# A decoder's attention, one head at a time, rewritten for pairs of heads

## The reference

```
moba (6 heads): softmax(q k^T / 8, causal) v          # with 256 tokens every key lies in the own block
nsa  (4 heads): g0 * softmax(q kc^T / 8) vc           # 15 compressed keys
              + g1 * softmax(q ks^T / 8, causal) vs   # all heads share one ks, vs
              + g2 * softmax(q kw^T / 8, causal) vw   # and one kw, vw
fox  (6 heads): softmax(q k^T / 8 + c_t - c_s, causal) v,  c = cumsum(log_sigmoid(f))
y = g_moba * (o_moba * silu(z)) W_moba + ... ;  x = x + y W_out
```

## Time and profile before

| | |
|---|---|
| runs | 2040.57 us median of 3 (2038.38 to 2041.07) |
| profiled execution | 2038.23 us, of which 2036.4 us from first to last instruction |
| PE busy | 1941.9 us (95%) |
| PE weight loads | 1804.3 us (89%) |
| DVE busy | 1271.0 us (62%) |
| ACT busy | 968.9 us (48%) |
| granted TensorE clock | 0.991 in the mean |
| HBM read | 299.30 MB |

### The profile page before, as it was taken

How to read it: one execution, slowest core, us unless ns; L and a number is a source line. 1 busy time by engine, 2 the same in 40 slices (tenths; PEclk the granted TensorE clock), 3 DMA queues, 4 the chain that set the end, 5 groups by cost and what they waited for, 6 DMA issues and landing times.

```text
span 2036.4 us, 35117 instructions
## 1 busy us (share of the span) xinstructions
PE 1941.9 (95%) x14810; PEld 1804.3 (89%) x14810; DVE 1271.0 (62%) x2087; ACT 968.9 (48%) x1481; POOL 79.2 (4%) x68
## 2 busy tenths in 40 slices
PE   7999997988999999999979889999999999999999
PEld 7999995887999999999868879999988779988779
DVE  6766575454666567665843646665764778753776
ACT  5544555244544444455552445444553544643542
POOL 0000101300000000000013000000000000000000
PEclk9999998999999999999989999999999999999999
DMA  8555431222555655554312325555446325446222
GB/s 319 187 185 187 156 125 62 81 96 94 176 186 182 207 182 186 183 187 156 117 63 82 105 84 176 185 184 187 158 146 205 97 72 170 155 153 202 87 76 101
DMA packets 84461, 302.63 MB, mean 149 GB/s; under 512 B 9168, under 2 KB 11728, under 8 KB 84176
## 3 DMA queue, kind: packets, MB, share of 16 engines
q1 hardware_dynamic: 84304, 300.39, 44.4%
HBM read 299.30 MB, written 1.05 MB: 147 GB/s over the span
## 4 chain that ended last, share of the span: by engine, by line
PE 88%; DVE 7%; ACT 2%; issue 2%; DMA 0%; SPq 0%; DVEq 0%; ACTq 0%
PE bank L383 22%; PE bank L387 22%; PE bank L386 22%; PE bank L663 3%; PE bank L401 2%; PE bank L404 2%; PE bank L405 2%; DVE w_lo L1458 1%; PE bank L843 1%; PE bank L956 1%; PE bank L448 1%; PE bank L452 1%; PE bank L453 1%; PE bank L778 1%; PE bank L921 1%
## 5 line engine op out<-in xcount | busy, mean ns | idle before, releaser
L383 PE MATMUL bank<-xs,w_hi 128*128 128x256 f32 x2576 | 737.8, 286 | 4.1 <-issue 4.1
L387 PE MATMUL bank<-xs,w_lo 128*128 128x256 f32 x2576 | 724.6, 281 | 0.0
L386 PE MATMUL bank<-xs,w_hi 128*128 128x256 f32 x2576 | 724.5, 281 | 0.0
L1031 ACT ACTIVATE w_hi<-ring 128x1024 fp32r<-128x1024 f32 x544 | 565.4, 1052 | 330.8 <-PE bank L383 258.7
L1458 DVE TENSOR_TENSOR w_lo<-ring,w_hi 128x1024 fp32r<-128x1024 f32 x544 | 653.5, 1235 | 103.9 <-ACT w_hi L1031 103.0
L383 PEld LDWEIGHTS bank<-xs,w_hi 128*128 128x128 f32 x2576 | 487.9, 189 | 24.4 <-issue 20.5
L386 PEld LDWEIGHTS bank<-xs,w_hi 128*128 128x128 f32 x2576 | 487.9, 189 | 3.2 <-issue 2.9
L387 PEld LDWEIGHTS bank<-xs,w_lo 128*128 128x128 f32 x2576 | 487.7, 189 | 0.0
L383 PE MATMUL bank<-a,w_hi 128*128 128x256 f32 x704 | 196.9, 280 | 0.0
L387 PE MATMUL bank<-a,w_lo 128*128 128x256 f32 x704 | 196.6, 279 | 0.0
L386 PE MATMUL bank<-a,w_hi 128*128 128x256 f32 x704 | 196.4, 279 | 0.0
(11 more groups left out here) (398 smaller groups left out, 3138.6 us busy)
## 6 DMA issues: line engine op xcount, KB each, us to landing
ring<-in_w SPq DMA_DIRECT2D x560, 512.0 KB, 3.3
arena<-in_mem SPq DMA_DIRECT2D x2, 1024.0 KB, 12.9
const<-in_const SPq DMA_DIRECT2D x1, 1647.0 KB, 16.2
h<-in_x SPq DMA_DIRECT2D x1, 768.0 KB, 7.5
out<-h SPq DMA_DIRECT2D x3, 256.0 KB, 2.3
dec_par<-in_dec SPq DMA_DIRECT2D x1, 615.0 KB, 19.9
h<-in_x SPq DMA_DIRECT2D x1, 256.0 KB, 3.9
out<-h SPq DMA_DIRECT2D x2, 128.0 KB, 1.9
```

The source lines that it names most:

```text
L383: last = nc.tensor.matmul(o, wh, hi(x, k0 + k), start=k == 0, stop=False, skip_group_check=True)
L386: nc.tensor.matmul(o, wh, lo(x, k0 + k), start=False, stop=False, skip_group_check=True)
L387: last = nc.tensor.matmul(o, wl, hi(x, k0 + k), start=False, stop=k == nk - 1, skip_group_check=True)
L1031: nc.scalar.activation(w_hi[:, s * UNIT:(s + 1) * UNIT], ring[:, u % RU, :], AF.Copy).then_inc(sems("w_hi"), 1)
```

## The change

The 20 units become 10 `PAIRED`, two heads each; nsa pairs share their keys.

- PE: `scores(i)` writes two neighbouring banks, first both heads' 256-key part and then both heads' 128-key part. For fox, four passes of rounded float32 over 64 rows add the forget sums (`rows_r` picks one head's row of `forget_r`, its high part in one group of 32 partitions and its low part in the next). Then two passes with the identity as stationary add the causal mask in PSUM. `turn` writes the turned weights over the scores in the same banks, both heads. `values` writes both halves of one bank, the two heads alternating. Scores of pair i wait until the turned weights of pair i-2 are copied. One filler step comes before `turn`, the others after it, and `values(i-1)` follows in the same iteration (before, it came one later). The compressed weights are turned in two visits, i = 1 and 4, in bank 7. `forget_rows` goes.
- ACT: one copy of both heads' turned weights (768 columns) first, then four exponentials straight out of PSUM with the scale 0.125, then `ptc`, high parts, tanh. Three copies per layer make the rounded constants; the copy of the forget sums has 256 columns instead of 12.
- DVE: no pass from PSUM to `s2`; two maxima over both heads straight out of PSUM, one sign, one reciprocal, two multiplications over both heads with a broadcast factor. Ahead of the loop four small scalings of the log forgets per layer, one memset in the first, and two subtractions of 32 partitions by 256 columns between `gates(1)` and `kcn`.
- POOL: its 18 operations per layer go. No DMA is added or removed but for a constant table that is smaller by 120 columns.

The names of semaphores are dealt out anew (left out here), the mask's sign is turned round, and a table `two32` is added to the constants. Lines that only "..." stands for are those removed, which the listing above shows, and unchanged ones.

```diff
@@ -194,7 +195,8 @@
-        bank = [ctx.enter_context(nc.psum_tensor(f"bank{i}", [P, 512], F32)) for i in range(8)]
+        banks = ctx.enter_context(nc.psum_tensor("bank", [P, 8, 512], F32))
+        bank = [banks[:, i, :] for i in range(8)]
@@ -319,6 +321,7 @@
+        forget_r = rounded("forget", T, arena_at + 4 * at[0])
@@ -326,14 +329,17 @@
+        mx2, nm2, sm2, rc2 = take(2, 4), take(2, 4), take(2, 4), take(2, 4)
+        gf, gate, xg, lf, lf2 = take(2, 18), take(2, 12), take(2, 6), take(2, 6), take(2, P)
...
+        p2, pt2 = take(2, 2, TRI), take(2, 2, TRI)
+        ident_r, causal_r, rows_r = (rounded(f"attend{n}", n, arena_at + 4 * (at[0] + o))
+                                     for o, n in ((0, P), (P, T), (P + T, 6 * P)))
+        take(7 * P + T)
@@ -882,10 +888,11 @@
+                nc.tensor.matmul(bank[4][:, 0:P], lf2[:, 0, :], le, start=True, stop=True, skip_group_check=True)
+                nc.tensor.matmul(bank[4][:, P:T], lf2[:, 0, :], ones, start=True, stop=False, skip_group_check=True)
+                nc.tensor.matmul(bank[4][:, P:T], lf2[:, 1, :], le, start=False, stop=True,
@@ -908,85 +915,99 @@
                         if j >= NH - 2 and t == 1:
                             last.then_inc(*pe.tell('cs_full'))
                 filler()
...
+                pe.e.wait_ge(*pe.need('masks', 3))
                 def scores(i):
...
+                    kind, q, k, _, tile = PAIRED[i][:5]
+                    b = 2 + i % 2 * 2
                     if i >= 2:
...
+                        pe.e.wait_ge(*pe.need('pt', i - 1))
+                    if i == 1:
+                        pe.e.wait_ge(*pe.need('fcol', 2))
+                        pe.e.wait_ge(*pe.need('kcs_ln', 1))
+                    Q, K = qn[:, q, :], qn[:, k, :]
+                    for t in (1, 0):
+                        for u in range(2):
+                            o = u * 64
+                            nc.tensor.matmul(bank[b + u][:, (1 - t) * T:(1 - t) * T + P + t * P],
+                                Q[o:o + 64, t * P:(t + 1) * P], K[o:o + 64, 0:P + t * P], start=t == 1, stop=False,
+                                skip_group_check=True)
+                    if kind == "fox":
+                        for t in range(2):
+                            for u in range(2):
+                                o, head = u * 64, (2 * (tile - 5) + u) * P
+                                nc.tensor.matmul(bank[b + u][:, t * T:(t + 1) * T], rows_r[o:o + 64, head:head + P],
+                                    forget_r[o:o + 64, :], start=False, stop=False, skip_group_check=True)
+                    for u in range(2):
+                        last = nc.tensor.matmul(bank[b + u][:, P:TRI], ident_r[:, :], causal_r[:, :], start=False,
+                            stop=True, skip_group_check=True)
+                    last.then_inc(*pe.tell('s_full'))
+                def turn(i):
+                    b = 2 + i % 2 * 2
+                    pe.e.wait_ge(*pe.need('pn', 2 * i + 2))
+                    for u in range(2):
+                        p = p2[:, i % 2, u, :]
+                        for c, at_ in ((T, 0), (0, P), (P, T)):
+                            last = nc.tensor.transpose(bank[b + u][:, at_:at_ + P], p[:, c:c + P], ident)
+                    last.then_inc(*pe.tell('t_full'))
+                def turn_compressed(j):
+                    pe.e.wait_ge(*pe.need('pcn', 1))
                     if j:
...
+                        pe.e.wait_ge(*pe.need('ob', 2))
+                    for u in range(2):
+                        for t in range(2):
+                            last = nc.tensor.transpose(bank[7][0:NCMP, u * T + t * P:u * T + (t + 1) * P],
+                                pc[:, 4 * j + 2 * u + t, :], ident)
+                    last.then_inc(*pe.tell('ct_full'))
                 def values(i):
...
+                    kind, _, _, vcols, tile, first, last = PAIRED[i]
+                    if i == 1:
+                        pe.e.wait_ge(*pe.need('ptc', 1))
                     pe.e.wait_ge(*pe.need('pt', i + 1))
                     b = 6 + tile % 2
...
+                    if tile >= 2 and first:
                         pe.e.wait_ge(*pe.need('ob', tile - 1))
...
+                    v, half = fv if kind == "fox" else v2, [bank[b][u * 64:u * 64 + 64, :] for u in range(2)]
                     if first and kind == "nsa":
...
+                        pe.e.wait_ge(*pe.need('ptc', 2))
+                        for u in range(2):
+                            nc.tensor.matmul(half[u][:, 0:T], vc[0:NCMP, :], ptc[0:NCMP, 2 * (tile - 3) + u, :], start=True,
+                                stop=False, skip_group_check=True)
+                    for t in range(2):
+                        for u in range(2):
+                            end = nc.tensor.matmul(half[u][:, t * P:T], v[:, t, vcols[u]:vcols[u] + 64],
+                                pt2[:, i % 2, u, t * T:t * T + T - t * P], start=t == 0 and first and kind != "nsa",
+                                stop=t == 1 and last, skip_group_check=True)
+                    end.then_inc(*pe.tell('o_full' if last else 'o_part'))
+                n = len(PAIRED)
+                for i in range(n + 1):
                     if i < n:
                         scores(i)
...
+                    steps = gate_steps(i + 1) - gate_steps(i)
+                    filler(1)
+                    if i >= 1:
                         turn(i - 1)
...
+                    filler(steps - 1)
+                    if i in (1, 4):
+                        turn_compressed(i // 4)
+                    if i >= 1:
+                        values(i - 1)
+                up_banks = (2, 3, 4, 5)
                 for m, (j, br, _) in enumerate(UPS):
                     first, nk = UP_TILES[br]
                     pe.e.wait_ge(*pe.need('ob', first + nk))
                     if m >= 4:
                         pe.e.wait_ge(*pe.need('up_out', m - 3))
...
+                    project(pe, w, ob, nk, up_banks[m % 4], "up_full", k0=first)
                 for j, b in enumerate(OUT_BANKS):
                     if j < 2:
                         pe.e.wait_ge(*pe.need('gl_e', 11 + j))
@@ -1304,6 +1325,9 @@
+                for r, c in ((ident_r[:, :], ident), (causal_r[:, :], C("causal")),
+                             (tiles(rows_r[:, :], 6), spread(C("two32")[:, 0:6], P))):
+                    nc.scalar.activation(r, c, AF.Copy).then_inc(*a.tell('masks'))
@@ -1346,7 +1370,7 @@
+                nc.scalar.activation(forget_r[:, :], bank[4][:, 0:T], AF.Copy).then_inc(*a.tell('forget_hi'))
@@ -1364,29 +1388,28 @@
                 a.e.wait_ge(*a.need('pc_d', 1))
                 nc.scalar.activation(pc, pc, AF.Exp).then_inc(*a.tell('pc_e'))
                 s.ahead(u0 + U_GL + 8)
...
+                n = len(PAIRED)
                 for i in range(n + 1):
...
                     if i >= 1:
...
+                        j, b = i - 1, 2 + (i - 1) % 2 * 2
                         a.e.wait_ge(*a.need('t_full', j + 1))
                         if j >= 2:
                             a.e.wait_ge(*a.need(*used_pt(j - 2)))
...
+                        nc.scalar.activation(pt2[:, j % 2, :, :], banks[:, b:b + 2, 0:TRI], AF.Copy).then_inc(*a.tell('pt'))
+                    if i < n:
+                        s_, b = i % 2, 2 + i % 2 * 2
+                        a.e.wait_ge(*a.need('nm', i + 1))
+                        for u in range(2):
+                            for t in (1, 0):
+                                x, k = slice((1 - t) * T, (1 - t) * T + P + t * P), 2 * t + u
+                                nc.scalar.activation(p2[:, s_, u, x], bank[b + u][:, x], AF.Exp, bias=nm2[:, s_, k:k + 1],
+                                    scale=0.125, accum_out=sm2[:, s_, k:k + 1]).then_inc(*a.tell('p'))
+                    if i in (1, 4):
+                        j = i // 4
+                        a.e.wait_ge(*a.need('ct_full', j + 1))
+                        nc.scalar.activation(ptc[0:NCMP, 2 * j:2 * j + 2, :], tiles(bank[7][0:NCMP, :], 2),
+                            AF.Copy).then_inc(*a.tell('ptc'))
+                    s.ahead(u0 + U_GL + 8 + gate_steps(i + 1) // 2)
                     for j in range(gates_turned(i), gates_turned(i + 1)):
                         gate_tanh(j)
                 for j in range(gates_turned(n + 1), 12):
@@ -1841,7 +1862,13 @@
+                    op1=ALU.subtract).then_inc(*d.tell())
+                if l == 0:
+                    nc.vector.memset(lf2, 0.0).then_inc(*d.tell())
+                d.e.wait_ge(*d.own())
+                for c in range(4):
+                    nc.vector.tensor_scalar(lf2[:, :, 32 * c:32 * c + 6], lf, -8.0, None,
+                        ALU.mult).then_inc(*d.tell('lf' if c == 3 else None))
@@ -1860,6 +1887,10 @@
+                d.e.wait_ge(*d.need('forget_hi', 1))
+                for o in (32, 96):
```

(27 more changed lines are left out.)

171 lines of the change are left out of this document (17 added, 154 removed).

## The result

The changed kernel takes 1977.47 us (median of 4 runs, 1974.92 to 1980.21) where the kernel before takes 2040.13 in the same comparison: a ratio of 0.9694, 95% interval 0.9677 to 0.9711, 62.7 us less. The profiled execution spans 1976.6 us against 2036.4, 59.8 less where my sum had 45.6; so 14 of the 17 us are looked for in the two traces (the other 3 are the distance between those two executions and the medians).

The account below looks back on a forecast made before the run. PE was taken to bound the kernel, attention stages included. Terms -32.4 - 6.3 - 2.3 + 0.4 + 1.2 - 6.2 = -45.6 from 2038.2 gave 1992.6, a median of 1995 us, range 1982 to 2016.

Parts of the forecast that it names:

- PE's waits: Attention stages, PE waiting for `turn` and `ptc`: 3.2 us per layer in place of 6.3, -6.2 us; bounds -12.6 to 0.
- pairs, forget sums, compressed keys, small transposes: PE's attention work: pairs -32.4 us, forget sums -6.3, compressed keys -2.3, small transposes in two visits +0.4.
- `kcn`: Two DVE subtractions between `gates(1)` and L1864 keep PE waiting: 0 to 0.8 us per layer, 0.6 taken, +1.2.
- all else outside the stages: Constants' copies, memset, small scalings, POOL and DMA: taken as 0; copies and scalings without cover 2 us per layer.
- The PE terms: PE's attention work: 2.74 us per pair of heads against 4.36, 1.62 less, 20 pairs, -32.4; without overlap -6.8.
- L905: Trace place with neighbouring products in two 64-row halves, read as two streams at full pace: 16 passes end in 1.09 us.
- The 0.21 that I worked out from it: First rival, passes start in program order: 0.21 us more for each `scores` and `values`, +9.3, 2004 us; chance 0.10.
- forecast of 1.0: Iterations 2 and 6: DVE's `gates` awaits ACT's high part, multiplications end 10.55, `turn` due 9.56; 1.0 us each.
- "0" for the constant table: Constants' copies ahead of PE: covered by units made ahead, so 0; the smaller table's shift of later tensors got no term.
- Everything outside the two stages within 2 us: Sign to check in the trace: outside the two attention stages, times would stay within 2 us of before.
- Rival 5: Attention ring through ACT and DVE, exponentials and maxima 1.6 times dearer from PSUM: +64, 2059 us, slower than before; chance 0.03.
- 6 us of waits off and 7 on: The main case's own range around its 1995 us, from PE's waits, given as 1987 to 2002.

## Why the prediction was right, and where it failed

The result, 1977.47, lies below the range, which ended at 1982. Two terms put it there: "PE's waits", 7.0 us too small, and the place of the operands, which I gave no price and which is worth some 8. Without the part of either that I missed, the time would have lain inside the range.

| term, us for both layers | forecast | from the traces |
|---|---|---|
| pairs, forget sums, compressed keys, small transposes | -40.6 | -40.6, a remainder (55.8 of the stages less 13.2 and 2) |
| waits of `turn` and `ptc` | -6.2 | -13.2 |
| the stages by the place of operands | 0 | about -2 |
| `kcn` | +1.2 | +1.9 |
| all else outside the stages | 0 | -6.0 in the profiled execution |
| sum | -45.6 | -59.9 (spans: -59.8) |

**The PE terms held.** The two choices that decided the size, full overlap of row halves (from L905) and of column halves (for which no row spoke), were right: 0.86 and 0.80 per pair where one head costs 0.84 and 0.79. That -40.6 comes out to the tenth is partly luck: it is a remainder, and what is taken off it is known to about 1 us; what holds is the terms per pair above. For the columns the forecast was a guess from the rows, and it came out. The passes start in pairs less than 0.01 us apart. The rule of the Trainium skill that I set against L905 says that matmuls start and end in program order ("TensorE: Matmul & The Clock Gate", section "Part 3: Packing small matmuls"). The 0.21 that I worked out from it for each `scores` and `values` is in neither trace. The records don't name the half of a pass or its place in the program, so they show that my working from the rule was wrong, and leave open what is in order.

**Failed: "PE's waits", the term of -6.2.** It went wrong at both ends. The old waits I took from the idle row, 6.3 per layer; from start to start they were 7.75, and the run with only DVE's order changed gave back 7.8. Idle time ahead of a matmul is not what the wait costs when the end of the pass before is modelled 0.16 us behind the next pass's usual start (0.28 us long, the next 0.12 behind it). The new waits I forecast at 3.2 per layer (two of 1.0 for `turn`, 0.3 for the last `turn`, 0.9 for `ptc`); they were 1.1 (0.29 for one `turn`, 0.84 for `ptc`). The mechanism in iteration 2 is as I described it, a gate projection between the exponentials and the multiplications, but each step is shorter. ACT and DVE there:

```profile
1597.44 0.48 ACT L1405 ACTIVATE arena<-bank,arena 128x256 f32<-128x256 f32 x1
...
1597.89 0.38 ACT L1405 ACTIVATE arena<-bank,arena 128x128 f32<-128x128 f32 x1
...
1598.23 2.02 ACT L1052 ACTIVATE w_hi<-ring 128x1024 fp32r<-128x1024 f32 x2
1599.34 1.22 DVE L1479 TENSOR_TENSOR w_lo<-ring,w_hi 128x1024 fp32r<-128x1024 f32 x1 [1.93 <-ACT w_hi L1052]
...
1600.48 0.68 DVE L1885 TENSOR_TENSOR arena<-bank,rstd 128x512 f32<-128x512 f32 x1
...
1601.09 0.17 DVE L1936 RECIPROCAL arena<-arena 128x4 f32<-128x4 f32 x1
1601.29 1.03 DVE L1945 TENSOR_TENSOR arena<-arena 128x512 f32<-128x512 f32 x2
```

A part of 256 and one of 128 columns take 0.79 from start to start (1597.44 to 1598.23), so four take 1.58, where I took 1.8 to 2.0; the reciprocal and the multiplications 1.14 (1601.09 to 1602.23, where the maxima start) instead of 1.35 with the gate. Instructions on ACT and DVE start up to 0.1 us before the one ahead has ended by its row (the four exponentials add up to 1.70 and take 1.58, the reads of their row sums included), and I had added durations whole. Iteration 2 begins at 1592.53. Its exponentials end 5.7 behind that instead of 6.25 and the multiplications 9.8 instead of 10.55, while `turn` was due at 9.55, as I had said. So the forecast of 1.0 became 0.29 in iteration 2 and nothing in iteration 6. Together the waits are 7.0 of the 14.3 that my sum was short.

**Failed: "0" for the constant table.** I mentioned among the DMAs that it gets smaller, and gave it no price. That it moves every operand behind it was in the diff and nowhere in the sum. The sign that I had named, "Everything outside the two stages within 2 us", failed: it was 6.0 apart from `kcn`. The kernel before, moved by 32 bytes, is 9.0 us faster, and its stages 0.4 and 0.6 shorter with waits 0.4 and 0.6 longer, so 2 us by pace inside them. Measured from that kernel, at 512 bytes' distance, the rewrite itself gives 2029.24 - 1977.47 = 51.8 us, and my sum with the waits and `kcn` put right gives 45.6 + 7.0 - 0.7 = 51.9. By the ratios of the two comparisons the first figure is 53.6, so they agree within 2 us, and the 0.1 is luck. Outside the stages the profiled executions differ by 6.0 apart from `kcn`, where the moved kernel's trace has 8.5; the rest is within what one execution differs from the next (the changed kernel's encoder ends at 1432.0 in one and 1427.3 in the other). That a shift of 512 bytes changes nothing by itself was not tried, and since place isn't all that moves the decoder's pace, the 6.0 is the likely price of the place, not a shown one.

**`kcn`** I took at 0.6 per layer between 0 and 0.8; it is 0.9: the two subtractions (0.88 us together in the trace) start at 1567.13, when ACT's logarithm and exponential have ended (1567.05), so these cover none of them. **`ptc`** came out as said. Rival 5's assumption, dearer exponentials out of PSUM, had the wrong sign. One slip: my own range, "6 us of waits off and 7 on", is 1989 to 2002 around 1995, not 1987 to 2002.

## What to carry to other kernels

Two products that each use half of TensorE's rows or columns cost here as much as one (0.86 against 0.84 us, 0.80 against 0.79) when they stood next to each other in the queue and differed in their half; separated by a third product each paid in full. Before rewriting such a stage, look whether an engine in its loop takes new work ahead of the work that the bound engine waits for: turning that order round gave 14.7 us here without any rewrite. Price such a wait from start to start. A change that makes an early SBUF tensor longer or shorter moves all that lie behind it. Here 32 or 96 bytes of padding were worth some 0.5% of the kernel, so time both kernels with a few bytes of padding before an effect of that size is put down to the edit.

## What the runs showed that I had not expected

- In the encoder the pace of identical projection passes goes with the place of the tensors in all 16 traces: 183.5 to 189.2 us for the same 1588 passes. In the decoder the same passes in the same place also ran at 113 ns in one trace and 118 in another.
- Exponentials with a row sum were shorter out of PSUM than out of SBUF: 475 against 494 ns for 256 columns, 375 against 402 for 128. Their order and scale differ too, so the source is the likely cause and not a shown one.
- With PE as busy as in the layer before (0.77 us idle in each) the granted clock was 0.96 in one stage where the same work had 1.00: 3 us in that execution.
